# Reordering the seams of a three-part transformer kernel: last key group's scores first, splits moved ahead, squares summed in wide pieces

## The reference, cut to what matters

```
first block:  xn = rms(x); proj = xn @ w_in
              a = forgetting attention (8 heads of 128)(proj)
              b = sparse attention (compressed, selected, window)(proj)
              x += (sig(gate_a)*(a @ w_up_fox) + sig(gate_b)*(b @ w_up_nsa)) @ w_out
              x += (silu(rms(x) @ w_gate) * (rms(x) @ w_up)) @ w_down
second, i=0:  q,k,v,gate = rms(h) @ attn_w_in      # 16 heads, 8 key groups
              o = softmax(rope(rms q) rope(rms k)^T) v
              h += rms((o * silu(gate)) @ attn_w_out)
second, i=1:  q,k,v,gate,lr = rms(h) @ gla_w_in    # 4 heads, linear attention
              o = forward and backward decayed linear attention(q, k, v, lr)
              h += rms((rms(o) * silu(gate)) @ gla_w_out)
```

## Time and profile before

| what | us |
| --- | --- |
| median of 3 runs | 2507.05 (2506.99 to 2507.28) |
| the profiled execution, device time | 2511.03 |
| its span, first to last instruction | 2509.2 |
| PE busy in it | 2447.1 |
| DVE, ACT, POOL busy | 1474.3, 1185.3, 104.9 |

### The profile page before, as it was taken

How to read it: one execution, slowest core, us unless ns; L and a number is a source line. 1 busy time by engine, 2 the same in 40 slices (tenths; PEclk the granted TensorE clock), 3 DMA queues, 4 the chain that set the end, 5 groups by cost and what they waited for, 6 DMA issues and landing times.

```text
span 2509.2 us, 50639 instructions
## 1 busy us (share of the span) xinstructions
PE 2447.1 (98%) x19620; PEld 2395.1 (95%) x19620; DVE 1474.3 (59%) x2204; ACT 1185.3 (47%) x1666; POOL 104.9 (4%) x133
## 2 busy tenths in 40 slices
PE   7999999999999999999999999999998989999987
PEld 7999999999999999999999999999998979999987
DVE  6666867755665555455545565555654465765645
ACT  5555554433545444334433445544544355655542
POOL 2000000000011000000000001000000100000001
PEclk9999999999999999999999999999999989999999
DMA  6545884466666666666666657555544535645543
GB/s 232 164 160 164 234 214 110 121 171 173 179 186 184 184 186 192 186 177 188 181 197 177 188 160 218 144 164 142 158 131 124 160 97 152 169 132 137 151 135 101
DMA packets 750271, 415.19 MB, mean 165 GB/s; under 512 B 44368, under 2 KB 738640, under 8 KB 750160
## 3 DMA queue, kind: packets, MB, share of 16 engines
q1 hardware_dynamic: 749328, 411.29, 58.6%
q10 hardware_dynamic: 832, 2.36, 0.2%
HBM read 408.35 MB, written 2.10 MB: 164 GB/s over the span
## 4 chain that ended last, share of the span: by engine, by line
PE 90%; DVE 4%; ACT 2%; issue 2%; DMA 1%; POOL 0%; SPq 0%; ACTq 0%; DVEq 0%; POOLq 0%
PE ps_unit L253 26%; PE ps_unit L251 26%; PE ps_unit L252 26%; DVE w_lo L238 1%; ACT w_hi L231 1%; PE ps_score L1018 1%; PE ps_out L863 1%; POOL work L2531 0%; PE ps_norm L863 0%; DVE work L354 0%; PE ps_score L585 0%; PE ps_score L586 0%; DVE work L2462 0%; PE ps_score L842 0%; PE ps_turn L842 0%
## 5 line engine op out<-in xcount | busy, mean ns | idle before, releaser
L238 DVE TENSOR_TENSOR w_lo<-raw,w_hi 128x1024 fp32r<-128x1024 f32 (+1 forms) x756 | 885.5, 1212 | 236.0 <-ACT w_hi L231 235.7
L231 ACT ACTIVATE w_hi<-raw 128x1024 fp32r<-128x1024 f32 (+1 forms) x776 | 784.6, 1042 | 429.4 <-PE ps_unit L253 426.1
L251 PE MATMUL ps_unit<-b_hi,w_hi 128*128 128x256 f32 (+1 forms) x3184 | 911.0, 286 | 5.9 <-DVE w_lo L238 5.9
L253 PE MATMUL ps_unit<-b_hi,w_lo 128*128 128x256 f32 (+1 forms) x3184 | 906.0, 285 | 0.0
L252 PE MATMUL ps_unit<-b_lo,w_hi 128*128 128x256 f32 (+1 forms) x3184 | 904.4, 284 | 0.0
L251 PE MATMUL ps_unit<-a_hi,w_hi 128*128 128x256 f32 (+1 forms) x2768 | 786.8, 284 | 5.4 <-DVE w_lo L238 3.1
L252 PE MATMUL ps_unit<-a_lo,w_hi 128*128 128x256 f32 (+1 forms) x2768 | 780.6, 282 | 0.0
L253 PE MATMUL ps_unit<-a_hi,w_lo 128*128 128x256 f32 (+1 forms) x2768 | 780.5, 282 | 0.0
L251 PEld LDWEIGHTS ps_unit<-b_hi,w_hi 128*128 128x128 f32 x3184 | 601.9, 189 | 11.9 <-DVE w_lo L238 5.5
L253 PEld LDWEIGHTS ps_unit<-b_hi,w_lo 128*128 128x128 f32 x3184 | 602.5, 189 | 0.0
L252 PEld LDWEIGHTS ps_unit<-b_lo,w_hi 128*128 128x128 f32 x3184 | 599.7, 188 | 0.7
(11 more groups left out here) (373 smaller groups left out, 1657.2 us busy)
## 6 DMA issues: line engine op xcount, KB each, us to landing
raw<-in_attn_w_in SPq DMA_DIRECT2D x96, 512.0 KB, 5.0
raw<-in_gla_w_in SPq DMA_DIRECT2D x96, 512.0 KB, 4.7
raw<-in_w_in SPq DMA_DIRECT2D x88, 512.0 KB, 4.8
raw<-in_w_ffn_gate SPq DMA_DIRECT2D x88, 512.0 KB, 4.6
raw<-in_w_ffn_up SPq DMA_DIRECT2D x88, 512.0 KB, 4.6
raw<-in_w_fox SPq DMA_DIRECT2D x64, 512.0 KB, 4.2
raw<-in_w_ffn_down SPq DMA_DIRECT2D x64, 512.0 KB, 4.7
raw<-in_w_out SPq DMA_DIRECT2D x32, 512.0 KB, 4.7
```

Of the source, the lines that this page charges most:

```text
L231: act.activation(hi[:, b % 4, 0:size], raw[:, b % 8, 0:size], ACT.Copy)\
L238: dve.tensor_tensor(lo[:, b % 4, 0:size], raw[:, b % 8, 0:size], hi[:, b % 4, 0:size], ALU.subtract).then_inc(lo_ready, 1)
L251: pe.matmul(dst, wh, xh[:, k0 + k, 0:N], start=start and k == 0, stop=False)
L253: mm = pe.matmul(dst, wl, xh[:, k0 + k, 0:N], start=False, stop=stop and k == kb - 1)
```

## The change: what it does, and the diff

1. **Start.** Seven matmuls on a zeroed tile run before the first real one. The two first units run four chunks at a time, one unit after the other, instead of chunk by chunk in turn. POOL's sixteen additions are gone; ACT's squares go to three buffers, and DVE adds them in five instructions: three of 1024 columns, one of 512, one of 256. The next unit (`U_FOX+1`) gets a PSUM bank of its own (`psS[1]`), so it doesn't wait for an evacuation, and `pe_norm` lies between its two blocks. `hi` and `lo` of its second block and of the block after move ahead of `act_norm`.
2. **Gated attention, exit.** The norm of the last key group, its swap and its rotation come one unit earlier on DVE. The scores come ahead of the first half of `U_AO`; the second halves are cut in parts (`mm_part`): six of eight chunks of one unit before the values, of the other after them, and the last two chunks of each at the end. The two `hi` and `lo` of `U_AO+1` go apart from each other, into gaps of ACT and DVE.
3. **Linear attention, entry.** `hi` and `lo` of `U_GL+5` go ahead of the norm, and the unit gets `psO` as its bank.
4. **Heads.** DVE adds two of the four squares to the other two (512 columns), and `gl_ssqs` has two matmuls instead of four. One combined table load stands ahead of the wait in `gl_rootf` and ahead of that in `gl_logsig`.
5. **Exit.** `hi` and `lo` of `U_GO+1` go around the norm of the last head, ahead of its split; the first turn of the output loops is written out, with the next `hi` and `lo` (`U_GO+2`) in its first slot.

```
-        def mm_block(pe, U, h, n, i, xh, xl, k0, dst, N, kb=HB, w=P, start=True, stop=True, late={}):
+        def mm_block(pe, U, h, n, i, xh, xl, k0, dst, N, kb=HB, w=P, start=True, stop=True, late={},
+                     own=False):
             b = 2 * U + h
             pe.wait_ge(lo_ready, b + 2 * n * i + 1)
-            if h == 0 and U >= 2:
+            if h == 0 and U >= 2 and not own:
...
-        sq4 = [W[:, 0:4 * T].rearrange("p (k n) -> p k n", k=4),
-               W[:, 4 * T:8 * T].rearrange("p (k n) -> p k n", k=4)]
+        sq4 = [W[:, 4 * T * n:4 * T * (n + 1)] for n in range(3)]
...
         def gl_ssqs(pe, h):
-            pe.wait_ge(gl_sq, h + 1)
-            for e in range(4):
-                mm = pe.matmul(psS[0][:, 0:T], i2048, lsq[:, e], start=e == 0, stop=e == 3)
+            pe.wait_ge(gl_sq, 2 * h + 2)
+            for e in range(2):
+                mm = pe.matmul(psS[0][:, 0:T], i2048, lsq[:, e], start=e == 0, stop=e == 1)
             mm.then_inc(gl_ssq, 1)
 
+        def gl_add_squares(dve, h):
+            dve.wait_ge(gl_sq, 2 * h + 1)
+            dve.tensor_tensor(lsq[:, 0:2], lsq[:, 0:2], lsq[:, 2:4], ALU.add).then_inc(gl_sq, 1)
+
         def gl_rootf(act, h):
+            ln_exp_table(act)
...
+        def halves_lo(dve, U):
+            for h in range(2):
+                lo_block(dve, 2 * U + h)
...
         def gl_logsig(act, h):
 
+            ln_exp_table(act)
...
+            ga_scores(pe, GQ_KV - 1)
             pe.wait_ge(aq_lo, 4)
             mm_block(pe, U_AO, 0, 0, 0, AH, AL, 0, dst[0], TM, stop=False)
-            ga_scores(pe, GQ_KV - 1)
             pe.wait_ge(evacuated, U_AO)
             mm_block(pe, U_AO, 1, 0, 0, AH, AL, 0, dst[1], TM, stop=False)
             ga_turn(pe, GQ_KV - 1)
+            pe.wait_ge(aq_lo, GQ_KV - 1)
+            mm_part(pe, U_AO + 1, 0, AH, AL, HB, dst[0], 0, HB - 2, TM)
             ga_values(pe, GQ_KV - 1)
-            pe.wait_ge(aq_lo, GQ_KV - 1)
-            mm_block(pe, U_AO + 1, 0, 0, 0, AH, AL, HB, dst[0], TM, start=False,
-                     late={HB - 2: [(aq_lo, GQ_KV)]})
-            mm_block(pe, U_AO + 1, 1, 0, 0, AH, AL, HB, dst[1], TM, start=False)
+            mm_part(pe, U_AO + 1, 1, AH, AL, HB, dst[1], 0, HB - 2, TM)
+            pe.wait_ge(aq_lo, GQ_KV)
+            for s in range(2):
+                mm_part(pe, U_AO + 1, s, AH, AL, HB, dst[s], HB - 2, HB, TM)
...
-                    unit(5, TM)
-                    if not gates:
+                    if gates:
+                        unit(5, TM)
+                    else:
+                        mm_block(pe, U_GL + 5, 0, 12, 0, BH, BL, 0, psO[:, 0:TM], TM, stop=False, own=True)
+                        mm_block(pe, U_GL + 5, 1, 12, 0, BH, BL, HB, psO[:, 0:TM], TM, start=False)
                         gl_logits(pe, h, True)
...
+            hi_block(act, 2 * U_AO + 2)
             ga_silu(act, GQ_KV, 1)
+            hi_block(act, 2 * U_AO + 3)
+            ga_exp(act, GQ_KV - 1)
             ga_copy_v(act, GQ_KV - 1)
-            split_hi(act, U_AO + 1, 0, 0)
-            ga_exp(act, GQ_KV - 1)
...
+                if kc == KC - 2:
+                    hi_block(act, 2 * U_GL + 10)
+            hi_block(act, 2 * U_GL + 11)
             act_norm(act, 4, TM)
...
                     gl_rootf(act, h - 1)
                     if heads:
                         split(5)
+                    else:
+                        hi_block(act, 2 * U_GO + 2)
                     gl_silu(act, h, 3)
+                    if not heads:
+                        hi_block(act, 2 * U_GO + 3)
                 if heads:
-                    if not gates:
-                        split(5)
                     split(6)
...
             def y_slot(i, last):
+                first = isinstance(i, int) and i == 0
                 for s in range(4):
-                    if not (last and s == 3):
+                    if first and s < 2:
+                        if s == 0:
+                            split_hi(act, U_GO + 2, 4, 0)
+                    elif not (last and s == 3):
                         split_hi(act, U_GO + s + 1, 4, i)
...
+                    if j == GQ_KV:
+                        ga_normed(dve, ca, j - 1)
                     unit(0, gate(0))
                     split(2)
-                    ga_normed(dve, ca, j - 1)
+                    if j < GQ_KV:
+                        ga_normed(dve, ca, j - 1)
+                    else:
+                        ga_rope(dve, ca, j - 1)
                     unit(1, gate(1))
...
-            ga_rope(dve, ca, j)
-            split_lo(dve, U_AO + 1, 0, 0)
+            lo_block(dve, 2 * U_AO + 2)
             ga_min(dve, j)
+            lo_block(dve, 2 * U_AO + 3)
             ga_weights(dve, ca, j)
...
+            halves_lo(dve, U_GL + 5)
 
             dve_norm(dve, 4, TM)
...
+                    gl_add_squares(dve, h - 1)
                     unit(2, gl_gate(h, 2), T)
                     split(4)
                     unit(3, gl_gate(h, 3), T)
                     if heads:
...
-                        split_lo(dve, U_GO + s + 1, 4, i)
+                        if not (isinstance(i, int) and i == 0 and s < 2):
+                            split_lo(dve, U_GO + s + 1, 4, i)
+                        elif s == 0:
+                            split_lo(dve, U_GO + 2, 4, 0)
                         y_evac(dve, U_GO, i, s, T)
...
-            for kc in range(KC):
-                pe.wait_ge(c_lo, kc + 1)
+            pe.wait_ge(fcm_zero, 1)
+            for _ in range(7):
+                pe.matmul(psO[:, 0:T], fcm[:, 0:P], fcm, start=True, stop=True)
+
+            def first_units(s, w, kc):
                 h, k = divmod(kc, HB)
+                b = 2 * h + s
+                if s == 0:
+                    pe.wait_ge(c_lo, kc + 1)
+                if k == 0:
+                    pe.wait_ge(lo_ready, b + 1)
+                dst = psU[s][:, 0:T]
+                wh, wl = hi[:, b, k * w:k * w + P], lo[:, b, k * w:k * w + P]
+                pe.matmul(dst, wh, AH[:, kc, 0:T], start=kc == 0, stop=False)
+                pe.matmul(dst, wh, AL[:, kc, 0:T], start=False, stop=False)
+                mm = pe.matmul(dst, wl, AH[:, kc, 0:T], start=False, stop=kc == KC - 1)
+                if k == HB - 1:
+                    mm.then_inc(block_done, 1)
+
+            for n in range(4):
                 for s, w in ((0, LOW), (1, P)):
-                    b = 2 * h + s
-                    if k == 0:
-                        pe.wait_ge(lo_ready, b + 1)
-                    dst = psU[s][:, 0:T]
-                    wh, wl = hi[:, b, k * w:k * w + P], lo[:, b, k * w:k * w + P]
-                    pe.matmul(dst, wh, AH[:, kc, 0:T], start=kc == 0, stop=False)
-                    pe.matmul(dst, wh, AL[:, kc, 0:T], start=False, stop=False)
-                    mm = pe.matmul(dst, wl, AH[:, kc, 0:T], start=False, stop=kc == KC - 1)
-                    if k == HB - 1:
-                        mm.then_inc(block_done, 1)
-            pe.wait_ge(s_con, 16)
-            pe_norm(pe, 0, T)
+                    for kc in range(4 * n, 4 * n + 4):
+                        first_units(s, w, kc)
...
+                if first:
+                    mm_block(pe, *u[1][:1], 0, *u[1][1:], AH, AL, 0, psS[1][:, 0:T], T, stop=False, own=True)
+                    pe.wait_ge(s_con, 16)
+                    pe_norm(pe, 0, T)
+                    mm_block(pe, *u[1][:1], 1, *u[1][1:], AH, AL, HB, psS[1][:, 0:T], T, start=False)
+                else:
+                    mm_unit(pe, *u[1], AH, AL)
...
             def square4(n):
                 act.wait_ge(s_x[n], 16)
-                if n >= 2:
-                    act.wait_ge(c_acc, 4 * n - 4)
-                act.activation(sq4[n % 2], X[:, 4 * n:4 * n + 4, 0:T], ACT.Square).then_inc(c_sq, 4)
+                if n == 3:
+                    act.wait_ge(c_acc, 4)
+                act.activation(sq4[(0, 1, 2, 1)[n]].rearrange("p (k n) -> p k n", n=T),
+                               X[:, 4 * n:4 * n + 4, 0:T], ACT.Square).then_inc(c_sq, 4)
 
             for kc in range(KC):
                 act.wait_ge(s_x[kc // 4], 16)
                 act_chunk(act, kc, kc, V_ATTN, AH, T)
-                if kc in (3, 7):
-                    b = 0 if kc == 3 else 2
-                    hi_block(act, b, N_LOW)
-                    hi_block(act, b + 1)
-                    square4(kc // 4)
-                if kc in (11, 12):
-                    square4(kc - 9)
-                if kc in (11, 13):
-                    hi_block(act, 4 + (kc == 13))
+                if kc == 3:
+                    hi_block(act, 0, N_LOW)
+                    square4(0)
+                    hi_block(act, 1)
+                if kc == 7:
+                    hi_block(act, 2, N_LOW)
+                    hi_block(act, 3)
+                    square4(1)
+                if kc == 10:
+                    square4(2)
+                if kc == 11:
```

(107 more changed lines are left out.)

3 lines of the change are left out of this document (2 added, 1 removed).

## The result

The changed kernel took 2478.16 us (median, 2476.95 to 2478.57), the kernel before beside it 2507.16 (2506.99 to 2508.2): ratio 0.9876, interval 0.9864 to 0.9889, 29.0 us less. The forecast was 2477.3. The profiled execution of the changed kernel took 2478.49, its span 2476.7; the spans of the two profiled executions are 32.5 us apart, 3.5 more than the medians.

What follows compares the result with a forecast made beforehand. PE was taken as the bound, busy 98% of the span, with waits at seams and low-clock stretches. 6.8 + 7.0 + 5.9 + 3.5 + 9.0 less 2.4 is 29.8; 2507.05 - 29.8 = 2477.3 us, range 2473 to 2485.

Steps and rivals of the forecast that it cites:

- this distance: Runs' median of the kernel before lies 3.98 us under its profiled execution (2511.03); claimed to stay so, giving 2507.05 as base.
- Place 1: Start: without POOL's additions DVE's chunks take 0.48 us, third unit starts at 30.1 for 36.91; 6.8 us gained.
- The 2.3 us that the prediction counts for 24 matmuls: Start: 24 fewer real matmuls at low clock save some 2.3 us, but worth nothing since PE waits for chunks until 21.9.
- Place 2: Exit of gated attention: next unit at 1921.35 for 1928.33, 7.0 us gained, less 2.4 for a clock fall behind a new gap.
- a gap of 2.3 us: Profile row of a 2.3 us gap followed by clock 0.50; reason to count a fall behind the new 2.7 us gap.
- Rival (a): Exit of gated attention: no clock fall in the new gap; 32.2 us gained, 2474.9; chance 0.17.
- Place 3: Entry of linear attention: PE has no gap and no clock fall, unit ends at 2051.6 for 2057.45; 5.9 us gained.
- Places 4 and 5: Linear attention: four heads gain 0.86 us each, 3.5; at the exit PE runs through without the 4.5 us wait, 9.0.
- rival (c): Fillers' splits come late by as much as gained, gaps only change place; within 5 us of before; chance 0.03.
- Rival (b): One seam gives little: DVE still bounds the start, or a new gap brings low clock; 22 to 25 us gained; chance 0.30.
- Rival (d): Loop over heads: DVE's new wait for squares holds back evacuation and split, kernel slower, 2523 at 12 us later; chance 0.02.

## Why the prediction was right

**The sum.** 29.8 us were foretold, 29.0 were measured in the pair, and the experiments' sum is 31.8, as large as the distance of the medians in the later comparisons (2510.04, 2510.64 and 2509.84 for the kernel before, less 2478.1: 31.9, 32.5, 31.7). So the terms were together 2 us small, and the sentence "nothing suggests that this distance changes" failed: the first runs of before (2506.99 to 2508.2) lay in the lower part of what that kernel does (2504.45 to 2512.68), while the changed kernel stays within 2476.95 to 2478.57. The two errors cancelled; the hit to within 0.9 us is partly luck, the mechanism is not.

| place | predicted | pair of traces | undone alone |
| --- | --- | --- | --- |
| 1 start | 6.8 | 6.5 | 9.8 |
| 2 exit of gated attention | 7.0 - 2.4 | 6.6 | 4.3 |
| 3 entry of linear attention | 5.9 | 7.0 | 5.1 |
| 4 heads | 3.5 | 3.4 | 3.6 |
| 5 exit | 9.0 | 9.0 | 9.0 |

**Place 1.** Each step is there: chunks at 0.48, the last one from 21.5 to 22.0, norm at 26.9, next unit at 30.4 (30.1 foretold). That POOL's adding slowed DVE is shown by adding on POOL again (a chunk 0.91 for 0.48). The other parts of this place (the order of the two first units, the bank of its own, the splits ahead of the norm) weren't undone one by one, so how the 6.5 us divide among them is open. The extra matmuls are worth nothing, as put, and for the reason given: PE waits at either pace, until 11.24 without them and until 11.54 with them. The first matmuls are 0.21 us apart up to 10.4 us and 0.12 from 11.6 on in the run without the seven. The 2.3 us that the prediction counts for 24 matmuls at the low pace did not come: undoing costs 0.5, within the scatter. What the term lacks is a size: the fall behind the old gap of 2.04 us, 0, 1.5 and 2.75 us in three profiles. The prediction read the one profile in which it was absent and took it for the rule.

**Place 2.** Unit foretold at 1921.35 less the 6.8 of place 1: 1914.6, found at 1913.68, 3.25 behind the evacuation (1910.43), through `hi` and `lo` in a row, as worked out. The gap of 2.7 is 2.5 to 2.65, its fall came, and cost 1.5 instead of 2.4, since it was 3.4 us long. So in the pair of traces the term was 2.0 small, 6.6 for 4.6: 0.9 of it is the fall, and 1.1 the late swap of before, which lies between the anchors of places 1 and 2 but isn't part of the change. Undone alone, the place gives 4.3 for the 4.6 foretold. The row that the prediction took for a gap of 2.3 us has PE busy for 0.42 of it, so that gap was 1.9 to 2.0; the fall was rightly expected all the same. Rival (a), no fall, came in one of nine profiles that have this gap (the one with POOL busy), and is worth 1.5 there; in six the fall lasted 3.4 us, in two (without the seven matmuls, and the heads as before) 6.8.

**Place 3.** The mechanism holds (no gap, unit behind the last norm matmul at once). Against the profile it was worked out from, the term was 1.1 small: the unit starts 24.1 us behind the first matmul on the chunks, not 25.0 (the fall that the kernel before has at 2030 is missing), and takes 6.1 instead of 6.3. The size also depends on how long the fall of before lasts: 7.0 with 6.8 us, 4.55 in the trace with 3.4 us, 5.1 between medians. That 5.9 lies between these is partly luck.

**Places 4 and 5.** As worked out, to 0.1 us; the room of 0.5 us or more that rival (c) doubted was there. Rival (b) is refuted too: the new gap is the foretold one, and no other wait took a removed one's place. A low stretch in the start, which it feared, did come (3.4 us from 12.9), but it is over before the splits that count, and the third unit lies at 30.1 to 30.4 with it and without it, in all profiles of the new start but the one with POOL busy. Rival (d): DVE's new wait shows in no row of the heads.

## What to carry to other kernels

Where an in-order kernel is bound by PE, look at each seam for the split or norm that the next matmuls wait for, and for work that could stand there; the gains of such places add up, and each is read from one anchor. A gap of PE is worth its length plus, where PE is the bound, a fall of the clock that comes in some executions and not in others (0, 1.5 and 2.75 us of PE's time behind the same gap of 2.04 us here), so take a gap's price from several profiles, and a small baseline of three runs with its whole scatter. Moving adds from GpSimd to VectorE made VectorE's chunks faster here, 0.48 us for 0.95, where the two had been running side by side.

## What was not expected of the hardware

Behind the same gap of 2.04 us at 28.6 to 29.0 us the granted clock stayed at 1.00 in one execution and fell to 0.50 for 3.4 and for 6.8 us in two others. Across all these profiles every fall but the last at the end of the kernel lasted 3.4 or 6.8 us; where PE was the bound the shorter ones cost some 1.5 us and the longer one behind the old gap 2.75. Fewer gaps probably also mean less scatter: the kernel before varies by 8 us (2504.45 to 2512.68, 46 executions), the changed one by 1.6 (8 executions, and fewer show less of a range).

At the start the granted clock prints as 1.00 in every profile, also where the first real matmuls run at half pace: 0.21 us apart up to 15.99 us in the kernel before (15.16 in its second profile) and up to 10.35 in the changed one without extra matmuls, 0.12 apart from 16.15 (15.34) and from 11.59 on. With the extra ones the real ones are 0.12 apart from 8.35 on; the seven themselves take 631 ns a record in the median, two of the same shape at full clock (line 335, at 26.7 us) 378. So the start is read from the distance between matmuls, and the pace that the seven gained was worth nothing here, where PE waits for the weight split either way (until 11.54 with them, 11.24 without). Nor does it last: with them ahead, five of ten profiles of kernels with the new start show a fall at 11.6 to 13.3 us. The single profile without them shows none, which may be chance.
